# A decoder layer on one core: three slots instead of four in the ring of the weights, and one mixing unit kept in place

## The reference, cut to what matters

```python
h = rmsnorm(x, norm_mix)
proj = h @ w_in                                   # 1024 x 3584
u_s5, x_lru, y_lru, g_a, g_b = jnp.split(proj, SPLITS, axis=-1)
a_out = s5_branch(...)      # diagonal scan, then a gate z * sigmoid(z @ w_glu)
b_out = rglru_branch(...)   # convolution, gates, scan
merged = (jax.nn.sigmoid(g_a) * (a_out @ w_proj_a)
          + jax.nn.sigmoid(g_b) * (b_out @ w_proj_b))
x = x + merged @ w_out
x = x + peer(rmsnorm(x, norm_ffn), w_q, sub_keys, u_tab, v_tab)
```

## Time and profile before

| | |
|---|---|
| median of 3 runs | 3223.39 us (3219.34 to 3223.61) |
| the profiled execution | 3224.72 us, of which its span 3222.6 us |
| PE busy | 2719.0 us (84%) |
| DVE busy | 2492.5 us (77%) |
| POOL busy | 1234.3 us (38%) |
| ACT busy | 981.4 us (30%) |
| moved by DMA | 1242.28 MB, mean 385 GB/s |

### The profile page before, as it was taken

One profiled execution on the slowest core, in us unless ns is written; L12 is line 12 of the kernel. 1 busy time (PEld: TensorE's weight loads), 2 busy tenths in 40 slices (PEclk: granted clock), 3 DMA queues, 4 the chain that ended last, 5 costly groups with the idle time before them and its releaser, 6 DMA issues.

```text
span 3222.6 us, 31760 instructions
## 1 busy us (share of the span) xinstructions
PE 2719.0 (84%) x9312; PEld 1557.2 (48%) x9312; DVE 2492.5 (77%) x5858; ACT 981.4 (30%) x3008; POOL 1234.3 (38%) x1048
## 2 busy tenths in 40 slices
PE   7988988999979988988878989999888995666566
PEld 6874544565445545655344545656434542222122
DVE  6836898888679888887678988887668897666754
ACT  2112443232134432322134432322123442222223
POOL 0003444334333444433343443443244443545553
PEclk9999999999989999999989999998999998887789
DMA  4269999999999999999999999999999998999997
GB/s 138 87 211 378 418 412 417 408 390 418 418 417 401 420 420 417 391 395 419 419 420 419 389 419 413 387 418 368 417 394 420 419 404 319 421 407 422 421 421 327
DMA packets 200445, 1242.28 MB, mean 385 GB/s; under 512 B 27704, under 2 KB 28088, under 8 KB 67664
## 3 DMA queue, kind: packets, MB, share of 16 engines
q0 software_dynamic: 148608, 1082.20, 81.8%
q1 hardware_dynamic: 50160, 153.21, 12.6%
q10 hardware_dynamic: 1504, 4.85, 0.4%
HBM read 1235.62 MB, written 4.55 MB: 385 GB/s over the span
## 4 chain that ended last, share of the span: by engine, by line
DMA 42%; PE 27%; DVE 20%; issue 3%; ACT 3%; DVEq 2%; POOL 2%; ACTq 1%; POOLq 0%
DMA arena<-in_uv,arena 41%; PE psum L1831 14%; DVE arena L1475 9%; PE psum L1732 7%; DVE arena L1068 4%; DVE arena L1060 3%; ACT arena L734 2%; PE psum L1876 2%; POOL arena L693 2%; DVE arena L1316 1%; PE psum L1747 1%; PE psum L1888 1%; PE psum L1767 1%; PE psum L1713 0%; PE psum L1867 0%
## 5 line engine op out<-in xcount | busy, mean ns | idle before, releaser
L693 POOL DMA_INDIRECT arena<-in_uv,arena x1032 | 1230.4, 1192 | 1960.7 <-PE psum L1831 1351.0
L1831 PE MATMUL psum<-arena 128*128 128x512 f32 x3192 | 1590.6, 640 | 444.8 <-ACT arena L734 398.8
L1475 DVE CUSTOM_DVE_ANT_0 arena<-arena 128x1024 f32<-128x1024 f32 x1024 | 1239.6, 1225 | 522.7 <-DMA arena<-in_uv,arena 486.6
L1831 PEld LDWEIGHTS psum<-arena 128*128 128x128 f32 x3192 | 612.4, 200 | 1272.1 <-ACT arena L734 614.6
L734 ACT ACTIVATE arena<-arena 128x1 f32<-128x1 f32 (+6 forms) x2485 | 700.5, 313 | 1605.1 <-DVE arena L1475 1452.9
L1732 PE MATMUL psum<-arena 128*128 128x256 f32 (+1 forms) x2688 | 625.3, 388 | 12.0 <-DVE arena L1068 6.4
L1732 PEld LDWEIGHTS psum<-arena 128*128 128x128 f32 x2688 | 516.3, 193 | 143.4 <-issue 71.2
L1068 DVE SCALAR_TENSOR_TENSOR arena<-arena 128x1024 f32<-128x1024 f32 (+6 forms) x461 | 373.2, 815 | 56.0 <-ACT arena L734 24.5
L1060 DVE TENSOR_TENSOR arena<-arena 128x256 f32<-128x256 f32 (+9 forms) x832 | 284.4, 381 | 23.3 <-issue 1.2
L734 ACT ACTIVATE arena<-psum 128x256 f32<-128x256 f32 (+7 forms) x266 | 107.2, 414 | 546.7 <-PE psum L1732 470.2
L734 ACT ACT_TABLE_LOAD x116 | 148.8, 1283 | 4.0 <-PEq L2146 0.8
(11 more groups left out here) (99 smaller groups left out, 1022.0 us busy)
## 6 DMA issues: line engine op xcount, KB each, us to landing
arena<-in_w_in SPq DMA_DIRECT2D x112, 512.0 KB
arena<-in_w_q SPq DMA_DIRECT2D x68, 512.0 KB
arena<-in_w_ab SPq DMA_DIRECT2D x40, 512.0 KB
arena<-in_w_out SPq DMA_DIRECT2D x34, 512.0 KB, 9.5
arena<-in_uv,arena POOLq DMA_INDIRECT x1032
arena<-in_keys SPq DMA_DIRECT2D x17, 256.0 KB, 7.8
arena<-in_w_glu SPq DMA_DIRECT2D x16, 256.0 KB
arena<-in_x_tok SPq DMA_DIRECT2D x8, 512.0 KB
```

What stands on the lines that cost most here:

```text
L693: pool.indirect_dma_start(uvring[:, r], None, i_["uv"], bass.IndirectOffsetOnAxis(column, 0)).then_inc(uv_in[r], 16)
L1475: V.tensor_tensor_reduce(out=u, in0=u, in1=hn[i // (SLOT // 2)], scale=1.0, scalar=0.0, op0=ALU.mult, op1=ALU.add, accum_out=dots_[:, b % ...
L1831: ins = mm(PV[:, half], dg[:, PAIR * (b % 2) + k], uvring[:, place(c, i) % UV, at:at + 512], start=(i % (SLOT // 2) == 0), stop=(pe_slots( ...
```

## The change

The ring has three slots. The 512 KB that the fourth took are a home of `w_ab` 4 for the whole program: it is loaded once, in the first chunk, and neither in that chunk's second pass over `w_ab` nor in the later chunks again. So each load through the ring waits for the unit three places earlier instead of four. All of SBUF behind the ring lies 4 KB a partition lower, and the homes' end is where it was.

```diff
-RING = 4
+RING = 3
...
-RESIDENT = (("w_out", 2),)
+RESIDENT = (("w_out", 2), ("w_ab", 4))
```

## The result

The changed kernel took 3232.08 us (median of 22 runs, 3220.81 to 3241.82), the kernel before 3223.9 us beside it (22 runs, 3219.34 to 3231.0). The ratio is 1.0025, 95% interval 1.0017 to 1.0034: slower by 8.2 us, where +1.9 us was forecast. The time lies at the upper end of the range of 3218 to 3232 us. The first eight runs of the changed kernel, in the order of the record, take 3225 to 3227 and 3236 to 3237 us in turn; why is open, and only the first of them, one of the long ones, has a trace. The profiled execution took 3237.07 us. The page of the changed kernel, against the earlier trace rows: span and instructions, the queues (packets, MB, share of 16 engines) and the chain by engine.

What follows compares the result with a forecast made beforehand. PE and weight loads pace the first 250 us, full DMA engines the rest. The terms -4.2 + 2.4 + 0 + 3.7 = +1.9 us gave 3225.3 us, called no change, range 3218 to 3232 us.

Steps and rivals of the forecast that it cites:

- Traffic that goes: Three `w_ab` loads saved in chunks 2 to 4 gain 4.2 us; a fourth, in the first chunk, gains 0.
- First chunk: Ahead of the first gather, four tight rounds of loads each make PE wait 0.6 us more: 2.4 us.
- second rival: Tight loads of the first chunk take 5.5 us to land: 4.8 us more than the sum, 3230.1 us; 12%.
- fourth rival: Bytes leaving the first burst of gathers let the sixth gather land up to 4.9 us earlier: 3216.7 us; 7%.
- Landing of the `w_glu` load: In chunks 2 to 4 the fourth `w_glu` unit's load lands in 7.8 us, so PE waits about 4 us.
- third rival: The fourth `w_glu` load lands in 4.3 us, a 0.7 us wait and no last-chunk hole: 3221.6 us; 15%.
- Chunks 2 and 3: PE's 3.9 us wait at the fourth `w_glu` unit there costs 0, as DMA works on.
- first rival: The stall in chunks 2 and 3 isn't covered and DMA runs dry: 10.3 us more, 3235.6 us; 13%.
- Last chunk: At the fourth `w_glu` unit, a 2.5 us DMA hole plus 1.25 us of slow PE: together 3.7 us.
- All other units of the later chunks: Units of chunks 2 to 4 other than the `w_glu` ones have gathers' steps between them: 0 us.

Runs made afterwards that it cites:

- the repeats: The changed kernel run again without any edit: 3238.92 us, ratio 1.005, and 3232.82 us, ratio 1.0024, against the kernel before.
- pairs, last: The changed kernel, but in the last chunk alone two `w_glu` units share one slot and one load: 3224.96 us, ratio 1.0002.
- parked: The changed kernel, but `w_ab` 3, 5, 6, 7 of the first chunk are kept in gather slots not yet in use: 3229.48 us, ratio 1.0016.
- home loaded anew: The changed kernel, but `w_ab` 4 is fetched into its home again in chunks 2 to 4: 3234.77 us, ratio 1.0038.
- three slots alone: The changed kernel without the home of `w_ab` 4, so three slots and nothing kept in the freed 512 KB: 3236.65 us, ratio 1.004.
- pairs, all: The changed kernel, but in chunks 2 to 4 two `w_glu` units share one slot and one load: 3224.2 us, ratio 0.9998.
- pairs, middle: The changed kernel, but in chunks 2 and 3 alone two `w_glu` units share one slot and one load: 3229.98 us, ratio 1.0015.
- four slots with pairs: The kernel before (four slots, no home of `w_ab` 4) with paired `w_glu` loads in chunks 2 to 4: 3221.2 us, 0.9997; again 3223.07 us, 0.9985.

## Where the prediction was right and where it was wrong

Slower by over 0.2% had 18%, no change 75%. The ratio of 1.0025 is over that line, but its interval (1.0017 to 1.0034) reaches below it; the repeats gave 1.005 and 1.0024. The parts of the sum one by one:

- **Traffic that goes, -4.2 us: right in bytes, too large in time.** 36 loads of `w_ab`, 151.12 MB. Up to 2141 us, where two of the three loads have been saved, the drift from the first gather on is (table) +1.0, -0.7, -2.5 and -5.1 us in the changed kernel and +1.0 and +0.1 in "pairs, last" and "parked", which save and stall alike: -1.0 us on average. The kernels that stall and save nothing (home loaded anew, three slots alone) have +2.5 and -1.4. So two loads look like 1 to 2 us, where the sum had 2.8, and single traces scatter by more than that. By whole times three loads are 2.7 us. The term was too large, by 1.5 us perhaps; that is not settled.
- **First chunk, +2.4 us: right in size, partly by luck in its parts.** The first gather moved by 2.2 to 2.8 us in four traces (table), with landings of 3.75 to 4.8 us in the chains of the second trace for tight loads (4.3 taken), and 6.51 us for the query unit's in the first. But in the first trace PE's waits for weights ahead of that gather come to 2.2 us (0.60, 0.16, 0.63, 0.78) against 1.0 before (0.81, 0.23): that is 1.1 of the 2.1 us by which it moved. The home's load was put at 0 as traffic there, and that understates the home: without it the first gather is some 4 us later still, because it takes waits out of the tight rounds. The 5.5 us of the second rival were not needed. Behind the first gather the fourth rival's effect is seen, for a while: the next chunk's columns are asked for at 288.23 us instead of 262.39, and by 311 us the drift of the four traces is down to 0.3, -0.9, -1.2 and -0.4 us, which the kernels with four slots don't show; at 588 us it is back at 3.2, 1.7, 1.5 and 1.9. Bytes that come later cost the same later, as the prediction took it.
- **Landing of the `w_glu` load, 7.8 us: right, with some luck.** 7.6 and 7.9 us by PE's rows, and waits of 3.2 to 4.9 us in every three-slot kernel where the pair doesn't take them away. The keys, from which the 7.8 us came, themselves take 10.8 us (median) in the changed kernel, so the stand-in happened to fit. The third rival (15%) asked for a landing in 4.3 us and a wait of 0.7 us, and is refuted here. It was also what the Trainium skill's rule of turns between queues ("DMA: Bandwidth & Descriptors", section "Queues, rings and completion order") would have given; by the measurement, that rule alone doesn't tell how soon a load lands beside this stream.
- **Chunks 2 and 3, 0 us: right as far as can be told.** The DMA share stays at 1.01 and 1.02 through both waits, and kernels with these stalls and without ("pairs, all" and "pairs, middle": -2.2 and +0.1 us from the first gather to 2141 us, against the -1.0 above) are not to be told apart. By the timed runs some 2 us are not excluded. The first rival (13%), which gave nearly the measured time, got it for the wrong reason.
- **Last chunk, +3.7 us: the mechanism was right, the size somewhat small.** The chain stall, half clock, late slot, hole is there step by step. The stall is 4.25 us (4.1 said). The half clock cost 3.38 - 1.83 = 1.55 us in the unit alone (1.25 said). POOL's gap grew to 13.8, 14.5, 14.1 and 14.4 us in the four traces, 6.2 to 6.9 us more than the 7.6 us, where the sum had a delay of 5.35. The first gather behind it also took POOL 1.73 us, where 0.94 is usual. In the hole 2.8 us were seen in the first trace, and 3.4 to 4.6 us in the other three, where 2.5 were forecast. On the table's clock this place costs 3.9 to 5.8 us, 5.2 on average; by 2713 us 0.7 of it is made good.
- **Around 2145 us, priced nowhere: a longer stretch at half clock.** PE waits 4.37 us for ACT there in every trace, the kernel before's too, and comes back slow. A group of L1831 behind it, in the changed kernel and in the kernel before:

```profile
2144.55 6.42 PE L1831 MATMUL psum<-arena 128*128 128x512 f32 x8
```

```profile
2141.71 3.71 PE L1831 MATMUL psum<-arena 128*128 128x512 f32 x8
```

  The granted clock is 0.50 from 2138 to 2150 us in the changed kernel, and in the kernel before 0.50 from 2138 to 2140 and 1.00 from 2142 us on; the DMA share falls to 0.77 from 2150 to 2160 us, where the kernel before keeps 1.01. The group takes 6.42, 6.48, 6.27 and 5.04 us in the changed kernel's traces, 6.3 to 6.4 in "home loaded anew", "pairs, middle" and "pairs, last", 5.03 in one trace of four slots with pairs, and 3.7 in the six others; in the same eight traces, and in no other, the drift jumps by 2.9 to 4.3 us there, of which part is made good by 2205 us. Since a kernel with four slots has it too, three slots alone hasn't, and the wait ahead of it is the same in all, it need not come from the change; why the slow stretch is longer in some traces is open.
- **The tail, 2713 to 2775 us, priced nowhere:** 1.2 to 6.6 us, 4.4 on average.

The forecast is 6.3 us short. The step that failed most is the one that put nothing where nothing waits for weights: "All other units of the later chunks have at least a step of gathers between two, and I take 0 for them". In its place the traces show a tail of 4.4 us on average and the longer slow stretch around 2145 us, both by causes that are open. The second is the size of "Together 3.7 us for the last chunk", where the table has 5.2 us, and the third the saving, which was taken too large.

Taking the last chunk's stall away alone brings 1.0025 to 1.0002, 0.0023 of 3224 us: 7.4 us by the timed runs, give or take 4 us by the two intervals. Against "pairs, middle", timed beside it, it is 5.0 us. Some 2.6 us of the 7.4 may be what pairing gives without any stall (the kernel before with pairs); what is left, 4.8 us, agrees with the 5.2 us seen on the spot.

The mean steps of the four traces are +2.5 to the first gather, -1.8 to 2141 us, +1.4, +5.2, -0.7 to 2713 us, +4.4 at the tail, +0.2 behind: 11.1 us, which is also how much the mean of the four spans (3235.0, 3236.8, 3227.1, 3228.5 us) exceeds that of the two of before (3222.6, 3218.9 us). The median of the timed runs, +8.2 us, is lower; the trace without the long tail wait ends at +6.3 us. So the saving is more than paid back: 2.5 us are spent ahead of the gathers and 5 us where the DMA engines have nothing queued behind the stall.

That the last chunk's units carry most of the loss is shown: pair their loads alone and 1.0025 becomes 1.0002. How much of that is the stall and how much the earlier loads is told only by the estimate above. That the pairs also clear the tail's wait (7.7 us in "pairs, last", 6.7 in "pairs, all") is seen, not explained; "pairs, middle", "parked" and "home loaded anew" keep the stall and have short tail waits (8.8, 11.7, 9.6 us), so the one does not force the other.

## What to carry to other kernels

The depth that this ring needs is set by the tightest run of units, not by the mean: with a landing time of 7.6 us and units of 1.8 us, the fourth load of a run of four needs its own slot or must ride with a neighbour's. A stall of the same 4 us cost nothing that could be measured where the transfer queue is full behind it and 5 us where the queue is about to run empty, so price stalls by what is queued for the bound engine, place by place. Before a slot is traded for traffic, try a larger load in the same slots: pairing two 256 KB loads gave the ring of three back what the loss of the fourth slot had cost (ratio 0.9998).

## What the hardware showed that was not expected

- Twice the bytes cost a load little beside the gathers. From 700 to 2700 us in the changed kernel the 256 KB of `w_glu` land in 7.1 to 7.8 us (median 7.4), the 512 KB of `w_ab` in 6.8 to 11.0 us (median 8.5), against 4.3 us for 512 KB with little beside them. The keys, 256 KB too, take 10.9 us there, so size is not what sets it.
- After a wait of 3.2 to 4.9 us for the fourth `w_glu` unit's weights PE's eight rows took 2.4 to 3.9 us instead of 1.8, in all traces of kernels that have the wait, so the stall costs PE 4.4 to 6.9 us and not 4. The Trainium skill, "TensorE: Matmul & The Clock Gate", section "HAM oscillation — how this bites in real kernels", tells of the same pattern, an engine that waits on a transfer and resumes slow; this trace agrees. How long PE stays slow is not the same each time: behind one and the same wait of 4.37 us for ACT the clock was at 0.50 up to 2140 us in one trace and up to 2150 us in another.
- The DMA engines can be full at 154 GB/s, while small stores and resuming gathers are under way together. The wait for these stores was 15.0, 17.9 and 16.9 us in three of four traces of one and the same program and 7.4 us in the fourth. The runs of the changed kernel spread over 21 us (3220.81 to 3241.82), those of the kernel before over 12.
